# Gate/up tiles of an encoder's FFN: the DRAM round trip and VectorE's finishing work moved to later units

## What is computed

```
def swiglu(xn, w_gate, w_up, w_down):
    return (jax.nn.silu(xn @ w_gate) * (xn @ w_up)) @ w_down

for layer in range(DEPTH):
    xn = rms_norm(x, attn_norm[layer])
    x = x + mixer(xn, ...)
    x = x + swiglu(rms_norm(x, ffn_norm[layer]), w_gate[layer], w_up[layer], w_down[layer])
```

## Time and profile before

| | |
|---|---|
| three runs | 2124.39, 2124.4, 2128.62 us, median 2124.4 |
| the profiled execution | 2123.84 us, its span 2122.0 us |
| TensorE matmuls busy | 2086.1 us (98%) |
| VectorE busy | 1547.0 us (73%) |
| ScalarE busy | 1078.3 us (51%) |
| DMA of SP's queue | 445.15 MB, 67.4% of 16 engines' span |
| granted TensorE clock | full in all 40 slices |

### The profile page before, as it was taken

The page is one execution under the profiler, slowest core; times in us unless marked ns, Lnnn a source line. Parts: engine busy times, 40 slices in busy tenths (PEclk is TensorE's granted clock), DMA queues, the critical chain, the costliest instruction groups (busy, mean ns, idle before and its releaser), DMA issues.

```text
span 2122.0 us, 27159 instructions
## 1 busy us (share of the span) xinstructions
PE 2086.1 (98%) x9192; PEld 1710.8 (81%) x9192; DVE 1547.0 (73%) x2077; ACT 1078.3 (51%) x1404; POOL 76.4 (4%) x85
## 2 busy tenths in 40 slices
PE   9999999999999999999999999999999999999999
PEld 7888888877777788888888888888777777888887
DVE  5777677877888755665576776687877888558887
ACT  6565555545554444444455566455544555445453
POOL 0100011000000000000011000110000000000000
PEclk9999999999999999999999999999999999999999
DMA  8788666676666776656677774666676666775664
GB/s 277 220 272 256 194 212 205 199 227 209 211 213 200 224 228 198 189 189 206 194 232 248 226 222 149 204 203 209 198 222 214 198 218 207 234 221 190 221 200 153
DMA packets 250993, 450.62 MB, mean 212 GB/s; under 512 B 17808, under 2 KB 50704, under 8 KB 250896
## 3 DMA queue, kind: packets, MB, share of 16 engines
q1 hardware_dynamic: 248448, 445.15, 67.4%
q10 hardware_dynamic: 2448, 4.21, 0.5%
HBM read 421.76 MB, written 27.53 MB: 212 GB/s over the span
## 4 chain that ended last, share of the span: by engine, by line
PE 70%; DVE 12%; DMA 10%; issue 4%; SPq 2%; ACT 2%; DVEq 0%; ACTq 0%; POOL 0%
PE psum L765 12%; PE psum L768 12%; PE psum L766 12%; PE psum L890 10%; PE psum L892 10%; PE psum L891 10%; DMA w_raw<-in_w_up 4%; DVE w_lo L1397 4%; DMA block_dram<-turn_sb 4%; DMA w_raw<-in_w_down 2%; PE psum L819 1%; PE psum L833 1%; SPq L633 1%; DVE stages L1809 1%; DVE stages L1807 1%
## 5 line engine op out<-in xcount | busy, mean ns | idle before, releaser
L1397 DVE TENSOR_TENSOR w_lo<-w_raw,w_hi 128x1024 fp32r<-128x1024 f32 (+1 forms) x708 | 844.7, 1207 | 407.4 <-ACT w_hi L1008 403.5
L1008 ACT ACTIVATE w_hi<-w_raw 128x1024 fp32r<-128x1024 f32 (+1 forms) x708 | 737.9, 1049 | 784.6 <-PE psum L768 321.4
L890 PE MATMUL psum<-w_hi,xt_hi 128*128 128x512 f32 x1216 | 474.5, 390 | 4.9 <-DVE w_lo L1397 4.6
L891 PE MATMUL psum<-w_lo,xt_hi 128*128 128x512 f32 x1216 | 473.2, 389 | 0.0
L892 PE MATMUL psum<-w_hi,xt_lo 128*128 128x512 f32 x1216 | 473.1, 389 | 0.0
L890 PEld LDWEIGHTS psum<-w_hi,xt_hi 128*128 128x128 f32 x1216 | 228.2, 188 | 57.3 <-DVE w_lo L1397 10.1
L892 PEld LDWEIGHTS psum<-w_hi,xt_lo 128*128 128x128 f32 x1216 | 228.2, 188 | 47.6
L891 PEld LDWEIGHTS psum<-w_lo,xt_hi 128*128 128x128 f32 x1216 | 228.2, 188 | 46.9
L765 PE MATMUL psum<-w_hi,xt_hi 128*128 128x512 f32 x604 | 243.2, 403 | 0.4 <-DVE w_lo L1397 0.4
L765 PE MATMUL psum<-w_hi,ht_hi 128*128 128x512 f32 x608 | 240.6, 396 | 0.0
L768 PE MATMUL psum<-w_hi,ht_lo 128*128 128x512 f32 x608 | 236.8, 390 | 0.0
(11 more groups left out here) (217 smaller groups left out, 2075.6 us busy)
## 6 DMA issues: line engine op xcount, KB each, us to landing
w_raw<-in_w_gate SPq DMA_DIRECT2D x176, 512.0 KB, 4.4
w_raw<-in_w_up SPq DMA_DIRECT2D x176, 512.0 KB, 3.9
w_raw<-in_w_down SPq DMA_DIRECT2D x168, 512.0 KB, 4.8
w_raw<-in_cd_w_in SPq DMA_DIRECT2D x80, 512.0 KB, 4.3
w_raw<-in_ab_w_in SPq DMA_DIRECT2D x71, 512.0 KB, 4.6
block_dram<-turn_sb SPq DMA_DIRECT2D x40, 512.0 KB, 4.9
w_raw<-in_ab_w_out SPq DMA_DIRECT2D x32, 512.0 KB, 4.7
w_raw<-in_cd_w_out SPq DMA_DIRECT2D x32, 512.0 KB, 4.0
```

Source lines behind the costliest of these rows:

```text
L890: nc.tensor.matmul(acc, a_hi, b_hi, start=start, stop=False)
L891: nc.tensor.matmul(acc, a_hi, b_lo, start=False, stop=False)
L1008: nc.scalar.activation(w_hi[:, slot, 0:n, :], w_raw[:, slot, 0:n, :], ACT.Copy).then_inc(hi_ready, 1)
L1397: nc.vector.tensor_tensor(w_lo[:, slot, 0:n, :], w_raw[:, slot, 0:n, :], w_hi[:, slot, 0:n, :].bitcast(F32), ALU.subtract).then_inc(lo_rea ...
```

## The change

It moves work to other unit numbers. On SP the write goes from unit 9 to 11 and the read-back from 11 to 14; the high parts that ScalarE makes from it go from 11 to 14, VectorE's low parts from 12 to 15. This holds for all tiles, and for the first down tile, whose loop finishes tile 10. For twin tiles alone VectorE's gate additions go from unit 0 to 1, its up additions from 2 to 4, product and transpose from 3 to 6, ScalarE's silu from 2 to 3, and the combination (and ScalarE's copy for it) from 14 to 15. `gate_sums` gets a wait for the combination of its own tile.

```
-BLOCKS_AT, BACK_AT, SPLIT_AT = 9, 11, 12
+GATE_AT, SILU_AT, UP_AT, HIDDEN_AT = 1, 3, 4, 6
+BLOCKS_AT, BACK_AT, SPLIT_AT = 11, 14, 15
+COMBINE_AT = 2 * UP_SEVEN[-1] + 1 + RING
...
             def finish_up(layer, i, odd, twin, idx):
-                if idx == (2 if twin else 1):
+                if idx == (SILU_AT if twin else 1):
...
-                    if twin and idx == 2 * UP_SEVEN[-1] + 1 + LEAD:
+                    if twin and idx == COMBINE_AT:
                         act.wait_ge(seven_used, up_sum(layer, i, UP_QUADS - 1) + 2)
...
             def gate_sums(layer, i, odd):
                 pu = ph["up", layer]
+                dve.wait_ge(combined, up_combination(layer, i) + 2)
...
             def finish_up(layer, i, odd, twin, idx):
-                if twin and idx == 0:
+                if twin and idx == GATE_AT:
                     gate_sums(layer, i, odd)
-                if twin and idx == 2:
+                if twin and idx == UP_AT:
                     up_sums(layer, i, odd)
-                if idx == 3:
+                if idx == (HIDDEN_AT if twin else 3):
                     hidden(layer, i, odd, twin)
                 if idx == SPLIT_AT:
                     hidden_lo(layer, i)
...
-                    if twin and idx == 2 * UP_SEVEN[-1] + 1 + LEAD:
+                    if twin and idx == COMBINE_AT:
                         up_combine(layer, i, odd)
```

## The result

The changed kernel takes 2098.0 us (median of four runs, 2093.9 to 2103.1) against 2125.3: a ratio of 0.987, 95% interval 0.984 to 0.990. Its profiled execution took 2100.8 us, with a span of 2099.0 against 2122.0: 23 us less. The lines moved by two or three; L1399, L1827 and L892 of the kernel after are L1397, L1824 and L890 of the one before.

The account below looks back on a forecast made before the run. TensorE was taken to bound the kernel, its waits costing twin tiles 38 us. With 19.5 us still lost, the gain of 18.5 us takes the profiled 2123.84 us to 2105.3, a median of 2106 us; range 2093 to 2119.

Parts of the forecast that it names:

- Gap A goes: TensorE's wait before quad 0's second part (0.36 us idle in tile 6) vanishes, 1.5 us to spare; T is TensorE's tile start.
- rival of no room on VectorE: Load 5 lands over 0.9 us later than worked out and unit 6 waits: about 2112 us; chance 0.06.
- Load 10 at T + 14.8, load 11 1.2 us behind: SP's issue times in a twin tile, T its start on TensorE; load 11 at T + 16.0 instead of T + 17.4.
- Load 11 lands at X + 7.1: X is load 10's issue; landing at T + 21.9, TensorE at T + 29.0 against 27.87; one microsecond is worth 16 us.
- gap B: TensorE's waits in front of quad 1 (0.48 and 1.21 us in tile 6), set by load 11; gone as well: 2092, 0.12.
- Lost afterwards 19.5 us: Stall left in the sixteen twin tiles after the change, at 1.2 us a tile.
- The ceiling, 38 us: All the change can win: what TensorE's waits cost the sixteen twin tiles, 2.4 us a tile.
- The 0.48 us gaps go: TensorE's smaller waits in front of quad 1 (line 1397, 8 places, 4.6 us) vanish, as unit 10's splits come in time.
- The write ahead of load 11 as a price: On SP the write stands between loads 10 and 11 and delays what is behind it as a load does.
- Later combination: nothing: VectorE's combination at unit 15 costs nothing; it ends about 5 us before TensorE needs it at the next tile's unit 0.
- Later up additions: VectorE's up additions, 1.40 us the pair, go behind the weight sums, in the chain to unit 5's half split.

Follow-up runs that it names:

- e11: The changed kernel run once more, unaltered: 2096.9 us, ratio 0.988 to the kernel before.
- e10: Changed kernel with gate additions, silu and combination back at units 0, 2 and 14, up additions still at 4, product at 6: 2109.9 us, ratio 0.993.
- e1: Kernel before with only the DMA part: write at unit 11, read-back at 14, its use at 14 and 15: 2106.9 us, ratio 0.989.
- e6: Changed kernel with gate additions, silu, up additions and combination back at units 0, 2, 2 and 14, and the write at unit 10: 2083.2 us, ratio 0.980.
- e4: Changed kernel with the write at unit 10, ahead of both loads 10 and 11: 2085.7 us, ratio 0.981.
- e3: Changed kernel with the write at unit 12, behind loads 10 and 11: 2089.0 us, ratio 0.982.
- e8: Kernel before with the write at unit 7, read-back at 14, used at 14 and 15; VectorE's and ScalarE's other work untouched: 2093.0 us, ratio 0.984.
- e2: Changed kernel with write, read-back and its use back at units 9, 11, 11 and 12; only VectorE's and ScalarE's moves kept: 2136.2 us, ratio 1.004.

## Why the prediction was right

The forecast was 2106 us with 2093 to 2119, the result 2098.0: the forecast's mechanism, with one term too large, and with one piece of luck.

- *Gap A goes.* Right, and close in its numbers: weight sums forecast at T + 2.49, measured T + 2.49; half split done at T + 10.75, measured T + 10.63. Load 5 leaves at T - 2.1, forecast T - 2.2, but lands at T + 2.1 in tile 6, not by T + 1.6 (the sum as written gives T + 1.4), so 0.4 us of room were left and not 0.9. The rival of no room on VectorE came about in one tile: in tile 5 of layer 0 the weight sums start at T + 3.66, and TensorE stood 0.69 and 1.22 us there. In e11 the same tile starts them at T + 3.6. In e10 it is the rule.
- *Load 10 at T + 14.8, load 11 1.2 us behind.* Measured T + 14.69 and 1.09. (The terms as written, 10.75 + 2.79 + 1.18, give T + 14.72 where the prediction has 14.64; it changes nothing.)
- *Load 11 lands at X + 7.1.* This is the term that was mis-sized: X + 6.8 in the median tile. I took the middle between the write's landing plus 1.3 and load 9 of the kernel before; the lower of the two was right (in tile 6 the write lands at X + 5.6, load 11 1.1 us later). At 16 us for each microsecond this is worth 5 us. The luck is in the idle path. The prediction put it down to the read-back being gone, and said nothing of load 9. e1 has the read-back gone as well, and load 11 lands at X + 8.15 in the median tile. That load 9 has landed when load 10 goes out is the work of the product between splits 5 and 6, which no sentence of the prediction counts as a reason for it; with X + 8.15 the whole change would have won next to nothing in gap B.
- *Lost afterwards 19.5 us.* Measured 16.4 in the trace, 1.0 a tile on average but 0.2 to 0.9 in thirteen tiles and 2.0 to 2.6 in three; the forecast had every tile alike. Gain 18.5 forecast, 23.0 in the span. The other 4 us to the 27 us of the medians are no more than the spread of the runs, 9 us for the changed kernel. The profiled execution of e11 (2094.3 us) shows a part of that spread: tile 1 of layer 0 loses nothing there, and load 11 lands 6.6 to 6.8 us behind load 10 in all of tiles 2 to 8.
- *The ceiling, 38 us.* About right. e6 has no stall left in these tiles. Against it, from T of tile 1 to the second part of quad 1 in tile 8, the kernel before needs 40.8 us more in the two layers together and the changed kernel 16.7 us. So a gap costs 0.35 us beyond its idle time on average, not the 0.3 of tile 6.
- *The 0.48 us gaps go.* Right but for three: there were 8, and 3 are left (0.3 to 0.7 us), in tiles 1, 3 and 5 of layer 0, where load 11 landed 10.5, 8.1 and 7.6 us behind load 10.
- *The write ahead of load 11 as a price.* Right that it costs, and e4 shows how much: by the ratios 14 us. Right in part as to its place. I held "ahead of load 11" to be the fault; right behind it (e3) 10 of the 14 us come back, and ahead of both loads (e4), where it leaves 1.7 us sooner than in the changed kernel, all 14. The Trainium skill's rule on the order of semaphore increments (DMA: Bandwidth & Descriptors, Queues, rings and completion order) would have let a late write hold load 11. Here load 11 landed behind the write in all 14 tiles (2 to 8), by 1.0 to 2.6 us, so nothing contradicts the rule. But plain queueing would look the same, and no run here shows what the rule cost, if anything.
- *Later combination: nothing.* Wrong as to what it does. In this change it is needed because of the late up additions, as e10 shows together with the kernel before, e1 and e8. *Later up additions* stood in my chain with their 1.4 us, but as a part of what takes gap A away. I never asked what the chain would be without that one move: it would have been 0.7 us shorter.

Whether gap A's share and gap B's share can be told apart: e8 takes B alone (34.8 us below its kernel before), e6 takes both (44.5 us). The difference, 9.7 us, is about what gap A's 14 places cost, at 0.34 us of idle time and 0.3 to 0.35 us more each (9 to 10 us).

## What to carry to other kernels

When a stall has been traced to one late transfer, list everything that is under way with it, ahead and behind, and look for the time when little else is: a write sent 1.7 us sooner, ahead of both loads, was worth 3 us more than one moved behind them (e4 against e3). Moving work on an engine changes the spacing of the loads that its finished units release, so order on the engine and order on the queue can't be judged apart; one half of a change may be worth nothing, or less, without the other. And in a change of several moves, cost each with the others in place: here one of VectorE's and ScalarE's five moves undid 11 of 37 us.

## What the runs showed of the hardware that I had not expected

A load of 512 KB can be slowed by a write issued behind it in the same queue. Load 10 of tiles 2 to 8 took 3.5 to 3.7 us with nothing within 1.0 us behind it (e3), as a load alone does (load 9 there: 3.5 to 3.8), and 4.1 to 4.5 with the write 0.57 us behind (changed kernel). With another load 1.27 us ahead it took 4.4 to 5.0 without the write (e8) and 5.3 to 6.4 with it (e1). A 512 KB write to DRAM took 2.7 to 3.1 us from issue to landing when no transfer had been issued in the 2.7 us ahead of it (e2, e4, tiles 2 to 8), 4.8 to 5.5 with one load 0.57 us ahead (kernel before, and tiles 2 to 8 of the changed kernel), and with two loads ahead 6.0 to 7.1 (e1, 0.57 and 1.84 us ahead) or 4.9 to 6.8 (e3, 0.57 and 1.57 us ahead).
